# Thirty-two in place of sixteen dense-side tokens go through the experts by rows

## What is computed

```python
def block(xb):                      # 128 tokens
    q = (xb @ wq).reshape(128, 8, 2, 128)
    s = einsum('thpd,hpkd->thpk', q, sub_keys)
    s_top, i_top = lax.top_k(s, 16)
    ...                             # 16 best of the 16 x 16 sums of two halves
    g = softmax(best_s, axis=-1)
    act = gelu(einsum('thkd,td->thk', expert_u[experts], xb))
    return einsum('thk,thkd->td', g * act, expert_v[experts])
```

## Time and profile before

| | |
|---|---|
| median of 3 runs | 2411.23 us (2410.53 to 2413.74) |
| span of the profiled execution (first to last instruction) | 2411.4 us |
| TensorE busy | 2367.4 us, 98% of the span |
| VectorE busy | 1567.8 us, 65% |
| GpSimd busy | 1244.2 us, 52% |
| ScalarE busy | 945.5 us, 39% |
| moved by DMA | 526.14 MB, mean 218 GB/s |
| granted TensorE clock, mean | 0.998 of full |

### The profile page before, as it was taken

One profiled execution on the slowest core, in us unless ns is written; L12 is line 12 of the kernel. 1 busy time (PEld: TensorE's weight loads), 2 busy tenths in 40 slices (PEclk: granted clock), 3 DMA queues, 4 the chain that ended last, 5 costly groups with the idle time before them and its releaser, 6 DMA issues.

```text
span 2411.4 us, 35928 instructions
## 1 busy us (share of the span) xinstructions
PE 2367.4 (98%) x12892; PEld 2127.2 (88%) x12892; DVE 1567.8 (65%) x2831; ACT 945.5 (39%) x1488; POOL 1244.2 (52%) x704
## 2 busy tenths in 40 slices
PE   7999999999999999999999999999999999999998
PEld 4878887899999999999999999997777888888886
DVE  5258535689899999779999999892266225422201
ACT  4374333344455555333333333342353223332312
POOL 2305443337899999555555555444304444444443
PEclk9999999999999999999999999999999999999999
DMA  7227522327978898999999999943202222222231
GB/s 283 80 115 258 182 91 84 133 94 255 324 252 301 299 328 309 396 379 414 416 415 409 417 408 414 370 166 106 82 14 96 97 96 96 96 93 99 90 102 70
DMA packets 179613, 526.14 MB, mean 218 GB/s; under 512 B 18240, under 2 KB 70896, under 8 KB 178224
## 3 DMA queue, kind: packets, MB, share of 16 engines
q1 hardware_dynamic: 120928, 345.24, 39.7%
q0 software_dynamic: 43024, 159.14, 17.0%
q10 hardware_dynamic: 15552, 20.36, 2.4%
HBM read 474.93 MB, written 49.73 MB: 218 GB/s over the span
## 4 chain that ended last, share of the span: by engine, by line
PE 91%; DVE 3%; DMA 2%; issue 2%; POOL 1%; ACT 1%; SPq 0%; ACTq 0%; DVEq 0%; POOLq 0%
PE bank L1372 21%; PE bank L1374 21%; PE bank L1373 21%; PE pair L1373 6%; PE pair L1372 6%; PE pair L1374 6%; PE pair L1726 1%; POOL wlo L714 1%; DMA wraw<-in_w 1%; PE bank L1889 1%; PE pair L1513 1%; PE bank L1552 1%; PE bank L1539 1%; DMA act_dram<-actb 1%; PE pair L1664 1%
## 5 line engine op out<-in xcount | busy, mean ns | idle before, releaser
L714 POOL TENSOR_TENSOR wlo<-wraw,whi 128x1024 fp32r<-128x1024 f32 x303 | 740.4, 2446 | 761.1 <-ACT whi L856 760.2
L1372 PE MATMUL bank<-HH,whi 128*128 128x512 f32 (+1 forms) x2048 | 740.2, 361 | 9.5 <-DMA T<-in_keys 3.0
L1373 PE MATMUL bank<-HL,whi 128*128 128x512 f32 (+1 forms) x2048 | 735.8, 359 | 0.0
L1374 PE MATMUL bank<-HH,wlo 128*128 128x512 f32 (+1 forms) x2048 | 735.7, 359 | 0.0
L856 ACT ACTIVATE whi<-wraw 128x1024 fp32r<-128x1024 f32 x456 | 481.8, 1058 | 632.2 <-PE pair L1374 337.4
L1372 PEld LDWEIGHTS bank<-HH,whi 128*128 128x128 f32 x2048 | 385.0, 188 | 54.8 <-issue 5.7
L1374 PEld LDWEIGHTS bank<-HH,wlo 128*128 128x128 f32 x2048 | 384.5, 188 | 40.3
L1373 PEld LDWEIGHTS bank<-HL,whi 128*128 128x128 f32 x2048 | 385.0, 188 | 39.6 <-issue 0.5
L780 POOL DMA_INDIRECT VROW<-in_w,which x128 | 206.0, 1609 | 190.5 <-DVE YROW L2522 178.0
L2454 DVE TENSOR_TENSOR wlo<-wraw,whi 128x1024 fp32r<-128x1024 f32 x153 | 186.4, 1219 | 20.9 <-ACT whi L856 20.0
L773 POOL DMA_INDIRECT X<-in_u_rows,which x128 | 149.0, 1164 | 57.3 <-DVE dots L2296 32.6
(11 more groups left out here) (447 smaller groups left out, 3815.1 us busy)
## 6 DMA issues: line engine op xcount, KB each, us to landing
wraw<-in_w SPq DMA_DIRECT2D x456, 512.0 KB
gate_dram<-GS SPq DMA_DIRECT2D x24, 1024.0 KB
GJ<-gate_dram SPq DMA_DIRECT2D x32, 768.0 KB
act_dram<-actb ACTq DMA_DIRECT2D x108, 184.0 KB
AJ<-act_dram SPq DMA_DIRECT2D x108, 184.0 KB
adaw<-in_ada SPq DMA_DIRECT2D x32, 512.0 KB
ada<-in_ada SPq DMA_DIRECT2D x16, 512.0 KB, 14.2
NB<-in_nab POOLq DMA_DIRECT2D x4, 1024.0 KB
```

Source lines behind the costliest of these rows:

```text
L714: nc.gpsimd.tensor_tensor(wlo[:, slot, :, :].rearrange("p k c -> p (k c)"), wraw[:, slot, :, :].rearrange("p k c -> p (k c)"), whi[:, slot ...
L1372: pe.matmul(out_, ah, bh, start=first, stop=False, **kw)
L1373: pe.matmul(out_, ah, bl, start=False, stop=False, **kw)
L1374: return pe.matmul(out_, al, bh, start=False, stop=last, **kw)
```

## The change

`FT` goes from 16 to 32. The dense side shrinks to `SD` = 352 columns in both expert stages, the gate part to 88 steps, and the extra tokens have 4 partitions each (`FS` = 4), so `DOTS` is 160 on either side: 16 more fetches and dots on U, 16 more fetches and row additions on V. In `V_ROWS` the extra tokens' additions now come after every third tile, up to tile 95, in place of every seventh, up to tile 111. The gate part has 44 dots in place of 46 (`GATE_DOTS`), the tail 56 in place of 38 (`TAIL_DOTS`), the second stage 32 as before, at tiles up to 109 in place of 104. `U_POOL` stays 103.

```diff
--- before.py
+++ after.py
@@ -61,7 +61,7 @@
 NCOL = _c
 
 TD = TB - 1
-FT = 16
+FT = 32
 FS = P // FT
 SD = TD * P - FT
 STEPS = SD // 4
@@ -70,15 +70,17 @@
 GATE_IT = LEAD_IT + 1
 GATE_TILES = 60
 TAIL = P - 4 * GATE_IT - GATE_TILES
-U_POOL = 4 * GATE_IT + GATE_TILES + 3
+U_TAIL = 4 * GATE_IT + GATE_TILES + 3
+U_POOL = 103
 FETCH_AT = 13
 DOTS_TOP = (0, 6, 11, 11)
 TOP_DOTS = sum(DOTS_TOP)
-GATE_DOT = 2
-PSUM_DOTS = TOP_DOTS + STEPS // GATE_DOT
-U_DOTS = 112
+GATE_DOTS = 44
+PSUM_DOTS = TOP_DOTS + GATE_DOTS
+TAIL_DOTS = 56
+U_DOTS = PSUM_DOTS + TAIL_DOTS
 DOTS = P + FT
-V_DOT_TILES = [10 * m // 3 + 1 for m in range(32)][:DOTS - U_DOTS]
+V_DOT_TILES = [7 * m // 2 + 1 for m in range(DOTS - U_DOTS)]
 ACTS = (60, 100, 116, P)
 V_ROWS = [k for j in range(P) for k in ((j, P + (j + 1) // (FS - 1) - 1) if (j + 1) % (FS - 1) == 0 and (j + 1) // (FS - 1) <= FT else (j,))]
 KEPT = 108
@@ -516,6 +518,10 @@
 
             return min(8 * GATE_TILES * n // STEPS, 8 * GATE_TILES)
 
+        def gate_dots(q):
+
+            return GATE_DOTS * q // STEPS
+
         def dot_column(m):
 
             return m if m < PSUM_DOTS else P + m - PSUM_DOTS if m < PSUM_DOTS + FT else m - FT
@@ -809,16 +815,20 @@
                 if (lows - gate0 - 3) * STEPS // GATE_TILES + 1 == q:
                     lo(G0["U"] + lows, lows % R)
                     lows += 1
-                if q >= 2 * GATE_DOT and q % GATE_DOT == 0:
+                while fetched < R + TOP_DOTS + gate_dots(max(q - 2, 0)):
                     fetch_u(fetched)
                     fetched += 1
             for t in range(lows, U_POOL):
                 lo(G0["U"] + t, t % R)
-            for k in range(fetched, U_DOTS + R):
+                while fetched < R + PSUM_DOTS + (t - U_TAIL + 1) * TAIL_DOTS // (P - U_TAIL):
+                    fetch_u(fetched)
+                    fetched += 1
+            u_fetches = min(U_DOTS + R, DOTS)
+            for k in range(fetched, u_fetches):
                 fetch_u(k)
             for b in range(2):
                 pool.wait_ge(g_out[b], 64 * TD)
-            fetched = U_DOTS + R
+            fetched = u_fetches
             for n, k in enumerate(V_ROWS):
                 fetch_v(n)
                 if fetched < DOTS and k - R in V_DOT_TILES:
@@ -2443,7 +2453,7 @@
                     gate_sum(2 * q - 4)
                     gate_sum(2 * q - 3)
                 gates_hot(q)
-                if q % GATE_DOT == GATE_DOT - 1:
+                while dotted[0] < TOP_DOTS + gate_dots(q + 1):
                     dot()
             for h in range(2 * STEPS - 4, 2 * STEPS):
                 gate_sum(h)
@@ -2466,11 +2476,12 @@
                 v.wait_ge(w_known, i + 1)
 
             then(nc.vector.memset(kept0[:, :, SD:TD * P], 0.0))
-            v.wait_ge(w_lo, G0["U"] + U_POOL)
-            tail_dots = U_DOTS - PSUM_DOTS
-            for t in range(U_POOL, P):
-                lo(G0["U"] + t, t % R)
-                while dotted[0] < PSUM_DOTS + (t - U_POOL + 1) * tail_dots // (P - U_POOL):
+            for t in range(U_TAIL, P):
+                if t == U_POOL:
+                    v.wait_ge(w_lo, G0["U"] + U_POOL)
+                if t >= U_POOL:
+                    lo(G0["U"] + t, t % R)
+                while dotted[0] < PSUM_DOTS + (t - U_TAIL + 1) * TAIL_DOTS // (P - U_TAIL):
                     dot()
 
             def pw_product(j, slot, peeled=False):
```

## The result

The changed kernel takes 2437.86 us (median of 4, 2436.02 to 2440.32) against 2411.28 for the kernel before on the same chip: ratio 1.0107, interval 1.0093 to 1.0122, slower by 26.6 us. The profiled execution took 2436.02 us, 1.8 more than its span. With the same 1.8, the profiled execution of the kernel before took 2413.2 us (an estimate), 2 above its median; ahead of the prediction the span was taken for the time. The stages are not touched by that: the second stage ends at 1606.4 us before and 1632.5 after, 26.1 later. What follows is the same work in all kernels. It took 801.7 to 807.9 us in the twelve profiles (805.0 before, 801.7 after), and its stretches agree to 0.1 us of PE's work up to the last one, so some 5 us at the program's very end vary from execution to execution.

A forecast was written before the change was run, and what follows sets the result against it. From the gate part's end to V tile 95, PE and the DMA engines (415 GB/s) were taken to be at their limits together. Lead -4.5, gate part -10.5, tail and V tiles 0 to 95 +34, rest -5: +14, 2425 us, range 2400 to 2443.

The forecast's parts named there:

- the ring: Tail: loop of four `UROW` buffers through fetch, dot and next issue, about 2.4 us a dot; no term in the prediction.
- The step for tail and V tiles 0 to 95: Tail and V tiles 0 to 95 together: 220.3 MB at 415 GB/s, 531 us, 34 more (bounds 29 and 43).
- 352 columns in 0.1603 us: Expert matmuls on PE: 0.1603 us each instead of 0.1668, a tile 3.85 us, 0.157 less.
- The rival by which PE's pace stays: Expert stages: weight loads set PE's pace, so narrower matmuls bring nothing; 2443 us, chance 0.02.
- Lead, 4.5: Lead, 40 tiles before the gate part: 4.5 us gained of 6.3 offered, bounds 0 and 6.3.
- Gate part, 10.5: Gate part, 60 tiles: 10.5 us gained, bounds 8 and 12, with GpSimd becoming the tighter neighbour.
- A ceiling of 415 GB/s: Tail and V tiles 0 to 95: the DMA engines give at most 415 GB/s, bounds 408 and 419.
- The rival with no limit: Tail and V tiles 0 to 95: no queue limit, engines can give 440 GB/s; 2387 us, chance 0.15.
- V tiles 0 to 95 at 4.22 us a tile: V tiles 0 to 95: DMA engines allow 4.22 us a tile at 1.75 MB; VectorE alone allows 4.0.
- The tail at 415 GB/s: Tail: priced by bytes at 415 GB/s, with 18 more U fetches, 9.4 MB.
- The rival *waits add up: Tail and V tiles 0 to 95: late rows stop VectorE, mean rate falls to 400 GB/s; 2445 us, chance 0.12.
- V tiles 96 to 127, 5.0: V tiles 96 to 127: PE is the bound, 32 x 0.157 = 5.0 us gained.

The follow-up runs named there:

- Experiment 1: The changed kernel with the extra tokens' 16 added V rows (fetches and row additions) left out: 2424.44 us, ratio 1.0045.
- experiment 7: The changed kernel without the loads of stored activations (`AJ`) in the second stage, result wrong in value: 2431.97 us, ratio 1.0075.
- experiment 3: The changed kernel with both the 16 added V rows and the 16 added tail dots left out, 352 columns kept: 2393.8 us, ratio 0.9921.
- experiment 9: The changed kernel with ScalarE's gelu of tile 125 moved ahead of rounding V's first product at the first stage's end: 2437.6 us, ratio 1.0106.

## Why the prediction was right, and where it was off

The time (2437.9 for 2425, range 2400 to 2443) and the side were right. The cause named, bytes over a ceiling of 415 GB/s, holds in the second stage and for 19 of the tail's 32 us; the other 13 came from the ring and the tail's two ends, which had no term. The step for tail and V tiles 0 to 95 measured +45.1, outside its own bounds of 29 and 43, so the step itself missed. The total still lies inside the 2417 to 2441 that the forecast gave itself, since that upper end had also allowed for a lead without gain and a gate part with 8 us, and these two gave 16 together. Step by step:

- *352 columns in 0.1603 us*: right. In the second stage's rest (1503 to 1632) 806 matmuls start in 129.5 us, 0.1607. The rival by which PE's pace stays is out. By the rule of the Trainium skill (Perfetto Trace Analysis, Identifying the Most-Contended Engine) that the share of weight loads tells how full PE is, as the prediction applied it, 0.167 would have been left; this trace speaks against that.
- *Lead, 4.5*: 7, of which 0.9 lie ahead of it, since the first expert matmul starts at 518.9 us for 519.8. The other 6.1 are just inside the bound of 6.3. Picking ended at 672.7 and PE was there, with a gap of 0.17 us. The waits of VectorE for U rows went from 7.1 to 0.6 us:

```profile
DVE X L2306 <- DMA X<-in_u_rows,which: 0.6, 2, 0.5
```

- *Gate part, 10.5*: 9.0, in its bounds. GpSimd is busy 268 of 278 us, near the 270 named. That it became the tighter neighbour is not shown: `OG` waits 11.0 us for its offsets, where it waited 10.6 before.
- *A ceiling of 415 GB/s*: right, and the basis of the rest. Experiment 1 takes bytes away and time goes at the same rate; no slice of V tiles 0 to 95 exceeds 420 GB/s. The rival with no limit is out. The figures of 425 and 435 GB/s of the Trainium skill (DMA: Bandwidth & Descriptors, Bandwidth and Specifications) were not sustained with this mixture of 512 KB loads and rows of 4 KB. That page's limit of 358 GB/s for a core, which its section Bandwidth ties to both cores streaming, did not bind here: 415 were held for 397 us. VectorE's 4.0 us a tile was near: experiment 7 measured 4.08.
- *V tiles 0 to 95 at 4.22 us a tile*: 4.13, since the loads of the first tiles lay in the tail (164.91 MB / 96 = 1.72 MB a tile for 1.75). From 1206.4 us on it is 4.25 (1676 matmuls in 296.6 us).
- *The tail at 415 GB/s*: **this step failed**. The sum priced the tail by its bytes alone, 132 us; it took 145.4. The prediction had seen the loop ("one loop through the DMA engines") and gave it no term. What was missing: a fetch of 512 KB lands in some 8 us, so four buffers give about a dot per 2.4 us, 56 dots 133 us. To this comes an entry in which one load of weights took 21.5 us and PE was idle for 6.5, and an end in which PE does a last tile at half the clock. The tail is longer than either bound because they hold one after the other: the transfers up to 1000 to 1020 us, the ring from there. The rival *waits add up* had the right mechanism at the wrong place: it let the mean of both stretches fall to 400; it fell to 405, by 378 in the tail and 415 in V. Its 2445 was 7 too high, the forecast's 2425 was 13 too low, so by the time alone that rival was the nearer one.
- *V tiles 96 to 127, 5.0*: 2.9. PE's pace was right, but it is idle for 2.1 us in all.

What stays open: with eight buffers the tail still takes 138.3 us for 133 of bytes. GpSimd's wait for the stores and its full stretch behind it are the likely rest, which is argued and not shown; a version in which that wait is not needed was not tried. Nor was one with the tail's dots begun earlier.

## What to carry to other kernels

Price added fetches three ways: by bytes over the highest rate seen, by the engine that consumes them, and by (landing + use + issue) / buffers. The stage takes at least the largest of these, and more than any of them where they take turns, as in this tail (132 and 133, measured 145). A stage in which PE is full and transfers run at the highest rate of the whole trace has two bounds: there a narrower matmul gave 7.5 of its 20 us (experiment 3), while bytes were paid at their full price (experiment 1). And a long wait at a stage's end is worth removing only if the stage behind starts earlier by it on the engine that bounds that stage.

## What the runs showed of the hardware

- A DMA share near 1 does not mean that the transfers run at the ceiling: at 1040 to 1060 us the share is 0.91 with 322 GB/s, and with eight buffers 1.02 with 409. The share moved by 12%, the bytes by 27%.
- The granted clock was low behind gaps of PE. After 11 us of gaps at 1080 to 1100 us it is 0.50 of full from 1099.8 to 1105.8, the lower of the two levels (1.2 and 2.4 GHz), and the matmuls of 352 columns start 0.29 us apart, against 0.16 at 1106:

```profile
1099.79 0.63 PE L1382 MATMUL bank<-HH,whi 128*128 128x352 f32 x1 [7.17 <-ACT kept L1139]
1100.22 0.49 PE L1383 MATMUL bank<-HL,whi 128*128 128x352 f32 x1
1100.51 0.49 PE L1384 MATMUL bank<-HH,wlo 128*128 128x352 f32 x1
...
1106.43 0.33 PE L1382 MATMUL bank<-WH,whi 128*128 128x352 f32 x1
1106.60 0.32 PE L1383 MATMUL bank<-WL,whi 128*128 128x352 f32 x1
1106.76 0.32 PE L1384 MATMUL bank<-WH,wlo 128*128 128x352 f32 x1
```

  The tile took 6.6 us (1099.8 to 1106.4) for 3.85, so this gap cost more than its length on PE. In experiment 9, where it was gone, the time stayed the same.
- A single load of 512 KB took 21.5 us from its issue where the median of the tail is 7.6. It stands at the head of the chain shown for the tail, and PE was idle 6.5 us between 980 and 1000.
